# One-column bisection steps, two sparse tiles moved into the band loop, and memory tokens through a weight slot, in a float32 decoder layer

## What is computed

```python
rel = relu(einsum('bthd,bsd->bths', iqb, ik))
score = einsum('bths,bth->bts', rel, iwb) * idx_scale
score = where(causal, score, -inf)
_, sel = top_k(score, 256)            # per query: 256 of the admissible keys
logits = einsum('bthd,btnd->bthn', q, k[sel]) * scale
p = softmax(where(sel <= qpos, logits, -inf)); o = p @ v[sel]     # 8 heads, one K/V head
```

## Time and profile before

| what | us |
|---|---|
| median of 3 runs | 1677.18 |
| lowest and highest run | 1669.87, 1680.44 |
| the profiled execution's own time | 1673.26 |
| its span, first to last instruction | 1671.5 |
| TensorE busy in it | 1528.0 (91%) |
| VectorE busy in it | 925.2 (55%) |
| ScalarE busy in it | 469.0 (28%) |
| GpSimd busy in it | 536.8 (32%) |

### The profile page before, as it was taken

One profiled execution on the slowest core, in us unless ns is written; L12 is line 12 of the kernel. 1 busy time (PEld: TensorE's weight loads), 2 busy tenths in 40 slices (PEclk: granted clock), 3 DMA queues, 4 the chain that ended last, 5 costly groups with the idle time before them and its releaser, 6 DMA issues.

```text
span 1671.5 us, 20607 instructions
## 1 busy us (share of the span) xinstructions
PE 1528.0 (91%) x7720; PEld 1301.1 (78%) x7720; DVE 925.2 (55%) x1670; ACT 469.0 (28%) x995; POOL 536.8 (32%) x540
## 2 busy tenths in 40 slices
PE   7999865897769999999999999999999999999993
PEld 7887645787768998778887788888888888888872
DVE  7568987998966432494435733333333333333348
ACT  3115346765665662121210211111111111111110
POOL 5332223665510003331333153333333333333100
PEclk9999987988958999999999999999999999999997
DMA  5554431544501004211110121111111111110002
GB/s 220 195 178 131 139 133 57 172 144 139 149 29 39 14 1 164 95 45 51 51 51 1 76 76 51 51 51 51 51 51 51 51 51 51 51 51 25 1 1 101
DMA packets 61474, 128.97 MB, mean 77 GB/s; under 512 B 7104, under 2 KB 34240, under 8 KB 53696
## 3 DMA queue, kind: packets, MB, share of 16 engines
q1 hardware_dynamic: 44352, 100.39, 18.1%
q10 hardware_dynamic: 17024, 27.27, 4.6%
HBM read 100.37 MB, written 27.26 MB: 76 GB/s over the span
## 4 chain that ended last, share of the span: by engine, by line
PE 75%; DVE 15%; ACT 4%; issue 4%; DMA 1%; POOL 1%; ACTq 0%; DVEq 0%; POOLq 0%
PE banks L631 21%; PE banks L633 21%; PE banks L632 21%; PE banks L823 3%; PE banks L683 2%; PE banks L684 2%; PE banks L810 2%; DVE unread L1420 2%; ACT unread_wide L1000 2%; DVE h_buf L1721 1%; PE banks L832 1%; DVE trial L1396 1%; DVE bn L1707 1%; DVE h_buf L1730 1%; DVE h_buf L1832 1%
## 5 line engine op out<-in xcount | busy, mean ns | idle before, releaser
L617 POOL TENSOR_SCALAR w_hi<-raw 128x512 fp32r<-128x512 f32 x268 | 176.3, 685 | 1034.2 <-PE banks L633 768.7
L622 POOL TENSOR_TENSOR w_lo<-raw,w_hi 128x512 fp32r<-128x512 f32 x268 | 362.9, 1385 | 0.0
L1832 DVE TENSOR_TENSOR h_buf<-h_buf,banks 128x1024 f32<-128x1024 f32 x120 | 146.5, 1221 | 146.5 <-PE banks L633 146.5
L631 PE MATMUL banks<-w_hi,hid_hi 128*128 128x512 f32 x512 | 200.2, 391 | 9.2 <-DVE h_buf L1832 9.2
L631 PE MATMUL banks<-act_hi,w_hi 128*128 128x512 f32 x512 | 199.3, 389 | 1.7 <-DVE act_lo L1700 1.7
L633 PE MATMUL banks<-w_hi,hid_lo 128*128 128x512 f32 x512 | 199.9, 390 | 0.0
L632 PE MATMUL banks<-w_lo,hid_hi 128*128 128x512 f32 x512 | 199.8, 390 | 0.0
L633 PE MATMUL banks<-act_hi,w_lo 128*128 128x512 f32 x512 | 199.2, 389 | 0.0
L632 PE MATMUL banks<-act_lo,w_hi 128*128 128x512 f32 x512 | 199.2, 389 | 0.0
L1215 ACT ACTIVATE relu_buf<-banks 128x512 f32<-128x512 f32 x64 | 38.3, 598 | 547.7 <-PE banks L633 547.7
L1796 DVE TENSOR_TENSOR relu_buf<-relu_buf 128x512 f32<-128x512 f32 x64 | 45.2, 707 | 247.6 <-ACT relu_buf L1215 247.6
(11 more groups left out here) (175 smaller groups left out, 2843.3 us busy)
## 6 DMA issues: line engine op xcount, KB each, us to landing
raw<-w_up_dram SPq DMA_DIRECT2D x16, 1024.0 KB, 4.8
raw<-w_down_dram SPq DMA_DIRECT2D x16, 1024.0 KB, 4.9
q_tile<-qk_dram SPq DMA_DIRECT2D x176, 64.0 KB, 2.2
qk_dram<-q_hi ACTq DMA_DIRECT2D x28, 256.0 KB, 2.3
qk_dram<-roped ACTq DMA_DIRECT2D x28, 256.0 KB, 2.8
x_raw<-x_t_dram SPq DMA_DIRECT2D x8, 512.0 KB, 8.3
raw<-wk_mem_dram SPq DMA_DIRECT2D x4, 1024.0 KB, 5.5
raw<-wv_mem_dram SPq DMA_DIRECT2D x4, 1024.0 KB, 5.7
```

Source lines behind the costliest of these rows:

```text
L617: pool.tensor_scalar(w_hi[s][:, col], raw[c % 2][:, col], 1.0, 1.0, ALU.mult, ALU.mult)\
L622: pool.tensor_tensor(w_lo[s][:, col], raw[c % 2][:, col], w_hi[s][:, col].bitcast(F32), ALU.subtract).then_inc(w_ready, 1)
L631: pe.matmul(dst, lh, rh, start=(first and n == 0), stop=False)
L1832: dve.tensor_tensor(h_buf[:, t, :], h_buf[:, t, :], ring_l[n % 2][:], ALU.add)\
```

## The change

Four parts, made together.

**Small steps on one column.** Find and flip now work on one column each, with one tensor input; `trial` and `offset` are given as per-partition scalars and the constant as an immediate. `level` is gone for the wide bits (`offset` changes its sign and becomes the limit of the comparison), and so is the tile `bits`.

```diff
+            def find_refused(c, k, limit):
+                return dve.tensor_scalar(refused[:, c:c + 1], count[:, c:c + 1], limit, float(1 << k),
+                                         ALU.is_lt, ALU.mult)
-            def set_next(cols, k):
+            def set_next(c, k):
+                col = slice(c, c + 1)
                 if k == 0:
-                    return dve.tensor_tensor(trial[:, cols], refused[:, cols], trial[:, cols], ALU.bitwise_xor)
-                return dve.scalar_tensor_tensor(out=trial[:, cols], in0=refused[:, cols], scalar=bits[:, k - 1:k],
-                                                in1=trial[:, cols], op0=ALU.bitwise_xor, op1=ALU.bitwise_xor)
+                    return dve.tensor_scalar(trial[:, col], refused[:, col], trial[:, col], None, ALU.bitwise_xor)
+                return dve.tensor_scalar(trial[:, col], refused[:, col], trial[:, col], 1 << (k - 1),
+                                         ALU.bitwise_xor, ALU.bitwise_xor)
...
             def set_wide(k):
-                def weigh():
                     dve.wait_ge(wide_counted, (TOP_BIT - k + 1) * (N_SEL - WIDE))
-                    at["level"] = then(dve.tensor_tensor(level[:, wide], count[:, wide], offset[:, wide],
-                                                         ALU.add))
+                    for c in range(WIDE, N_SEL):
+                        at[c] = then(find_refused(c, k, offset[:, c:c + 1]))
                 def apply():
-                    set_next(wide, k).then_inc(trial_ready, 1)
+                    for c in range(WIDE, N_SEL):
+                        dve.wait_ge(dve_step, at[c])
+                        ins = set_next(c, k)
+                    ins.then_inc(trial_ready, 1)
```

```diff
+                def bisect(cols):
+                    waiting = None
+                    for k in range(top, -1, -1):
+                        for c in cols:
+                            cost, counted = narrow_tally(c)
+                            if waiting is not None:
+                                narrow_set(*waiting)
+                            waiting = (c, k, counted)
+                            yield cost + 0.3, None
+                    narrow_set(*waiting)
+                def bisect_alone(c, beside):
+                    for k in range(top, -1, -1):
+                        cost, counted = narrow_tally(c)
+                        yield cost + 0.3, None
+                        more = next(beside, None)
+                        if more is not None:
+                            yield more
+                        narrow_set(c, k, counted)
+                    yield from beside
...
+                yield from bisect((0, 1))
+                yield from bisect_alone(2, finish_narrow((0, 1)))
+                yield from finish_narrow((2,))
```

```diff
+N_BAND = NT + FIRST_TOPK_TILE
+BAND_HEADS = [(t, h) for t in range(N_BAND) for h in range(0, HEADS, PAIR)]
-DSA = [(i, h) for i in range(NT) for h in range(HEADS)]
+DSA = [(i, h) for i in range(FIRST_TOPK_TILE, NT) for h in range(HEADS)]
...
+WIDE_END = N_HALVES - 2
-    done = N_HALVES - WIDE_HALF
-    j = 2 * (n + 1) // 3
-    return TOP_BIT - done - j if n >= 0 and 3 * j // 2 == n and j <= TOP_BIT - done else None
+    done = WIDE_END - WIDE_HALF
+    j = (4 * n + 6) // 7
+    return TOP_BIT - done - j if n >= 0 and 7 * j // 4 == n and j <= TOP_BIT - done else None
-BUDGET_SWA = 1.5
+BUDGET_BAND, BUDGET_DSA = 1.8, 2.0
```

```diff
+                if c == C_MEM:
+                    sp.wait_ge(w_ready, PIECES * (c - 2))
+                    sp.dma_start(mem_raw(), a["mem_t"]).then_inc(mem_in, 16)
...
+                elif c == C_MEM + 1:
+                    sp.wait_ge(mem_lo_done, 1)
                 else:
-                    sp.wait_ge(w_ready, PIECES * (c - 2))
+                    sp.wait_ge(w_ready, PIECES * (c - 2 + (c == C_MEM)))
```

More of the change, by code:

```diff
@@ L1481, in select_keys @@
-                for step in small:
-                    step()
-                dve.wait_ge(dve_step, steps[0])
-                chain(dve.tensor_tensor(threshold[:, narrow], sign[:, narrow], trial[:, narrow].bitcast(F32),
-                                        ALU.mult))
-                for c in range(N_SEL):
-                    while c == WIDE and not wide_set[0]:
-                        yield 1e9, None
-                    if c == WIDE:
-                        dve.wait_ge(trial_ready, TOP_BIT + 2)
-                        found = plain[:, wide]
-                        chain(dve.tensor_scalar(found, trial[:, wide], SIGN_BIT, None, ALU.bitwise_xor))
-                        found = found.bitcast(F32)
-                        chain(dve.scalar_tensor_tensor(out=level[:, wide], in0=found, scalar=1.25 * 2.0 ** -24,
-                                                       in1=found, op0=ALU.mult, op1=ALU.add))
-                        for cc in range(WIDE, N_SEL):
-                            yield tally(cc, ALU.is_ge, level[:, cc:cc + 1], minus_rank[:, cc:cc + 1]), None
-                        dve.wait_ge(dve_step, written[-1])
-                        chain(dve.tensor_tensor(level[:, wide], level[:, wide], found, ALU.subtract))
-                        chain(dve.scalar_tensor_tensor(out=level[:, wide], in0=count[:, wide], scalar=0.0,
-                                                       in1=level[:, wide], op0=ALU.is_ge, op1=ALU.mult))
-                        chain(dve.tensor_tensor(level[:, wide], level[:, wide], found, ALU.add))
-                        chain(dve.tensor_tensor(threshold[:, wide], sign[:, wide], level[:, wide], ALU.mult))
@@ new lines, in select_keys, with narrow_tally, narrow_set @@
+                set_at = {c: steps[0] for c in range(WIDE)}
+                def narrow_tally(c):
+                    dve.wait_ge(dve_step, set_at[c])
+                    return tally(c, ALU.is_ge, trial[:, c:c + 1].bitcast(F32), minus_rank[:, c:c + 1]), written[-1]
+                def narrow_set(c, k, counted):
+                    dve.wait_ge(dve_step, counted)
+                    dve.wait_ge(dve_step, then(find_refused(c, k, 0.0)))
+                    set_at[c] = then(set_next(c, k))
+                def bisect(cols):
[8 more added lines that the diff above has]
+                    narrow_set(*waiting)
@@ new lines, in bisect_alone, with finish_narrow @@
+                def bisect_alone(c, beside):
[7 more added lines that the diff above has]
+                    yield from beside
+                def finish_narrow(cols):
+                    for c in cols:
+                        dve.wait_ge(dve_step, set_at[c])
+                        chain(dve.tensor_tensor(threshold[:, c:c + 1], sign[:, c:c + 1],
+                                                trial[:, c:c + 1].bitcast(F32), ALU.mult))
+                        yield from finish(c)
@@ L1529, in select_keys @@
                     yield width / 1700.0, i
+                yield from bisect((0, 1))
+                yield from bisect_alone(2, finish_narrow((0, 1)))
+                yield from finish_narrow((2,))
+                while not wide_set[0]:
+                    yield 1e9, None
+                dve.wait_ge(trial_ready, TOP_BIT + 2)
+                found = plain[:, wide]
+                chain(dve.tensor_scalar(found, trial[:, wide], SIGN_BIT, None, ALU.bitwise_xor))
+                found = found.bitcast(F32)
+                chain(dve.scalar_tensor_tensor(out=level[:, wide], in0=found, scalar=1.25 * 2.0 ** -24,
+                                               in1=found, op0=ALU.mult, op1=ALU.add))
+                for c in range(WIDE, N_SEL):
+                    yield tally(c, ALU.is_ge, level[:, c:c + 1], minus_rank[:, c:c + 1]), None
+                dve.wait_ge(dve_step, written[-1])
+                chain(dve.tensor_tensor(level[:, wide], level[:, wide], found, ALU.subtract))
+                chain(dve.scalar_tensor_tensor(out=level[:, wide], in0=count[:, wide], scalar=0.0,
+                                               in1=level[:, wide], op0=ALU.is_ge, op1=ALU.mult))
+                chain(dve.tensor_tensor(level[:, wide], level[:, wide], found, ALU.add))
+                chain(dve.tensor_tensor(threshold[:, wide], sign[:, wide], level[:, wide], ALU.mult))
+                for c in range(WIDE, N_SEL):
+                    yield from finish(c)
             pending = []
@@ L1681, in _ @@
                 if last >= 0 and last % HEADS == HEADS - 1:
-                    normalise(NT + last // HEADS)
+                    normalise(N_BAND + last // HEADS)
                 if n < NS:
@@ L1843 @@
           "wk_mem", "wv_mem", "wq_mem", "wo_mem", "w_o", "w_up", "w_down", "gamma", "beta",
-          "ident", "swa_mask", "causal", "inv_freq", "bits")
+          "ident", "swa_mask", "causal", "inv_freq")
 def k_tiles(w):
```

163 lines of the change are left out of this document (68 added, 95 removed).

## The result

The changed kernel takes 1656.38 us (median of 4 runs, 1650.68 to 1660.99), beside 1677.26 for the kernel before (4 runs, 1669.87 to 1680.44): a ratio of 0.9878, 95% interval 0.9838 to 0.9918. That is 21 us less; 1651 was forecast, within 1633 to 1672. The profiled execution took 1660.99 us, the highest of the four, with a span of 1659.2.

A forecast was written before the change was run, and what follows sets the result against it. VectorE, its small steps held by GpSimd, was taken to bound most of 256 to 512 us. Tile 4's first mask 25.6 us earlier gave 1673.3 - 25.6 = 1647.7; with 3.9 for the median, 1651, range 1633 to 1672.

The forecast's parts named there:

- The small steps: VectorE's bisection finds and flips: on one column with one input, stalls beside GpSimd go; VectorE gains 23 us.
- The wide step: Three finds and three flips per wide bit on VectorE: 29 us in 31 bits becomes 19.
- The narrow steps: Three narrow tiles' finds and flips: splitting columns adds 17 plus 3 us; 33 to 34 us of surplus go.
- the third rival: New small steps held by GpSimd like the old: 33 us of surplus stay, 1684, no change or slower; chance 0.06.
- the prediction's example: The worst small VectorE step took 4.40 us while GpSimd worked beside it without a pause on its splits.
- The start: Before band unit 6: first mask about 249, memory products 262 and 276, unit 6 at 282; 7 us at the start.
- The band units: 34 units from 6 to unit 40: VectorE 4.3 plus idle 0.7, 5.0 us each, 170 in all; unit 40 at 452.
- Idle: 0.7 again: Band units from 6 on: VectorE's idle time per unit stays at the 0.7 us it had before.
- the first rival: Stalls go, but ScalarE or TensorE binds: a band unit costs 5.5 us, only 9 us gained; chance 0.14.
- The sparse units: Units 40 to 47 take 26 us and 48 to 55 take 33; tile 4's first mask comes at 511.
- Behind it nothing changes: After tile 4's first mask, at 511 instead of 536.62, the rest takes as long as before: 25.6 us gained.
- The last sentence of the sum: 23 us VectorE, 7 start, 49 at causal units against 16 for eight more band units and 34 beside tiles 2 and 3.

The follow-up runs named there:

- two-input run: Changed kernel, but the flip reads refused and trial as tensors and the constant from bits, still one column at a time: 1676.72 us, ratio 1.0014.
- six bits beside the rope: Changed kernel with six wide bits beside the rope again, the sixth set ahead of unit 0: 1657.24 us, ratio 0.9903.
- the rotated one: Changed kernel, three narrow tiles bisected together, find one count later, flip two, estimate per count cost + 0.1 instead of + 0.3: 1648.13 us, ratio 0.9847.
- one in two: Rotated order with wide bits one in every two units instead of four in seven, the last at unit 52: 1647.48 us, ratio 0.9844.

## Why the prediction was right, and where it was not

**The small steps** were right in mechanism and in their total. 210 ns was taken for the flip, and 207 to 210 measured; 23 us were to be saved on VectorE, and the groups show 81.7 - 59.6 = 22 in that stretch, over the whole program 925.2 - 899.9 = 25.3. But its two terms were off in opposite ways, so that the agreement is in part luck. The wide step was to fall from 29 to 19 us, at 0.3 us for three finds and 0.3 for three flips, but three finds took 14.1 us in 31 bits, 0.45 each time, and three flips as much, so it stayed at some 28 us. The narrow steps saved the rest, some 21 us instead of 13. The two-input run shows what was held among the flips, and the third rival (the new steps held too) is out.

The Trainium skill (SBUF — State Buffer, section "Who interferes with whom") lets a tensor_scalar enter a two-port mode and be held, when its operands meet certain conditions; the old find on two columns was held (474 ns), none of the one-column ones was. Its other statement, that a hold lasts as long as the one instruction, fits most holds here: 62 of the 65 in the kernel before and all 59 of the two-input run took at most 1.4 us, about one split. It does not fit three of the kernel before, which took 3.62, 4.40 and 4.78 us, over three or four splits in a row. So the prediction's example was one of three exceptions and not the usual case.

**The start** was right to a microsecond or two at each of four markers. But its 7 us are not in the result as such: with six bits beside the rope they are lost at the first mask, and the time can't be told from that of the changed kernel.

**The band units** were mis-sized a little: 5.16 us each (175.55 us in 34) instead of 5.0. VectorE's part came to 4.05 us (137.87 in 34) instead of 4.3, its idle time to 1.1 instead of 0.7. "Idle: 0.7 again" is the term that failed: VectorE stopped being the engine that bounds, and a part of the saving turned into waits for scores (26.3 us, where 8.1 were before). That is the first rival's mechanism, at 0.16 us a unit instead of 0.5. Together 5.5 us over 34 units, and 1.4 from the start.

**The sparse units** came out at 26.6 and 31.6 us (26 and 33 were forecast). "Behind it nothing changes" failed: tile 4's units lost 5.3 us at the low clock, a stretch which the earlier trace rows shows at 1.00. The accounts of the profiled execution: 6.2 us late at tile 4, 5.3 more at tile 5, and 1.8 behind the last mask (1049.4 us from there to the end of the span, 1047.6 before) make the 13.3 us by which the span of 1659.2 lies above the forecast's 1645.9. Of the 1.8, some 0.9 arise between 938 and 949 us, where the changed kernel's granted clock is 0.79 (938 to 946) and was 1.00 in the same place before (952 to 960). The runs' median is only 5.4 us above the forecast, since this execution was the slowest of its four, while the profiled one of before lay below its median: the 3.9 us added for that in the sum went the other way.

**The attribution** is where the reasoning was weakest. The last sentence of the sum had four terms: VectorE's 23 us, the start's 7, and 49 us at the causal units given up for 50 elsewhere. They add up to 29 and not to the 25.6 that they were to explain. The first alone is the gain (21.5 us when made alone). I had costed pairs and the new order as one lump that evens out; the runs show two opposite effects in it, pairs at 4 to 20 us for it and the in-order selection, with its estimates, at 6 to 17 against it. The total was right because both stand in the code together, not because either was understood.

A version that beats both kernels is the rotated one, with four bits in seven (0.9847, 0.9815 to 0.9879) or one in two (0.9844, 0.9829 to 0.9859), 6 to 9 us below the changed kernel's two medians. Its slowest run with one bit in two, 1649.45, is slower than only one of the changed kernel's eight.

## What to carry to other kernels

Look at a group's mean against its own undisturbed length, not at how small the instruction is: steps of 0.2 us that average 0.5 beside a busy GpSimd can be the largest removable term, and giving them one tensor input on one column, with scalars for the rest, took the stall away although there are more of them. When several edits come together, cost each of them against the same base, since a sum that agrees can hide two effects of 10 us and more with opposite signs. And look where an engine has slack and where it is full: here the faster orders had done tile 4's counts beside the memory products, before the stretch in which the finishing fills VectorE.

## What the runs showed of the hardware

- Small VectorE instructions with one tensor input on one column, a per-partition scalar from SBUF among them, were not held by GpSimd in any group: means of 145 to 210 ns in hundreds of cases. The scalar operand adds some 60 ns (149 to 207).
- The same flip with two tensor inputs averaged 446 ns on one column: 754 where a GpSimd instruction ran at the same time, 216 where none did. A find with one input on two columns was held too (803 and 165).
- A hold ended with a GpSimd instruction each time (124 of 124 small steps over 300 ns). It mostly took one split (about 1.3 us) or less; three of the kernel before lasted over three or four splits in a row (3.62, 4.40 and 4.78 us). What sets those three apart is open.
- TensorE stayed at its low clock (1.2 GHz, granted 0.50) for more than 10 us while busy without a pause, in three profiles of one order of work, before it rose to 2.4 GHz; in the rotated kernel it was already high when the same units came, with TensorE idle for part of the time before. What decides it is open. It is worth 3 to 7 us here (20.5 us for tile 4's units against 17.8, 23.1 against 16.0).
- The eight executions of the changed kernel fall in the order of their mean granted clock: 1661.0, 1658.7 and 1658.5 us at 0.957, then 1656.8 (0.960), 1654.0 (0.961), 1651.1 and 1650.7 (0.963), 1649.1 (0.967). So its spread goes with the clock; in which stretch the clock was low is known only for the two profiled ones, 1661.0 and 1658.5.
